# PEER experts of a hybrid decoder step: five places for gathered rows, one raw buffer for U, the row of sums in the memory of the h row, splits of U at other places

## The reference

```python
e = i1 * N_KEYS + i2                      # expert of the token, head and place, of 128 * 128
g = jax.nn.softmax(cv, axis=-1)
a = jax.nn.gelu(jnp.einsum('td,thkd->thk', tb, u_tab[e]).astype(jnp.float32), approximate=False)
return jnp.einsum('thk,thkd->td', (g * a).astype(tb.dtype), v_tab[e])
```

## Time and profile before

| | |
|---|---|
| median of 3 runs | 3907.29 us (3895.41 to 3909.98) |
| the profiled execution's own time | 3909.41 us |
| its span, first to last instruction | 3907.8 us |
| TensorE busy | 3267.4 us (84%) |
| VectorE busy | 2644.8 us (68%) |
| GpSimd busy | 1591.6 us (41%) |
| ScalarE busy | 1348.8 us (35%) |
| mean granted TensorE clock | 0.929 |

### The profile page before, as it was taken

How to read it: one execution, slowest core, us unless ns; L and a number is a source line. 1 busy time by engine, 2 the same in 40 slices (tenths; PEclk the granted TensorE clock), 3 DMA queues, 4 the chain that set the end, 5 groups by cost and what they waited for, 6 DMA issues and landing times. The chain is left out here.

```text
span 3907.8 us, 58722 instructions
## 1 busy us (share of the span) xinstructions
PE 3267.4 (84%) x20561; PEld 2846.2 (73%) x20561; DVE 2644.8 (68%) x5883; ACT 1348.8 (35%) x3194; POOL 1591.6 (41%) x1343
## 2 busy tenths in 40 slices
PE   6999788566687975656699999999999999999994
PEld 3676455211277964555599999999999999999993
DVE  4224776110234799989688888888888888888885
ACT  3010566000221113879433323333323333333331
POOL 0010000000212444999645545545546455455450
PEclk8999899777788987888899999999999999999997
DMA  6632873999412122665688888888888888888883
GB/s 226 239 131 73 236 215 114 367 414 410 165 65 89 60 76 71 251 245 204 273 311 332 314 311 340 321 320 339 306 327 322 317 335 316 315 336 312 320 293 136
DMA packets 280369, 991.41 MB, mean 254 GB/s; under 512 B 21925, under 2 KB 139536, under 8 KB 215865
## 3 DMA queue, kind: packets, MB, share of 16 engines
q1 hardware_dynamic: 214648, 480.71, 34.0%
q0 software_dynamic: 62784, 469.88, 31.8%
q10 hardware_dynamic: 2752, 38.75, 2.6%
HBM read 909.52 MB, written 146.80 MB: 270 GB/s over the span
## 5 line engine op out<-in xcount | busy, mean ns | idle before, releaser
L2210 PE MATMUL e_pa<-k_hi_d,e_uh 128*128 128x320 f32 x2048 | 616.0, 314 | 77.7 <-DVE e_act L2371 62.1
L2211 PE MATMUL e_pa<-k_lo_d,e_uh 128*128 128x320 f32 x2048 | 605.5, 309 | 0.0
L2410 POOL DMA_INDIRECT e_uv<-peer_uv,k_g_idx x416 | 400.6, 963 | 498.2 <-DVE e_pY L2351 442.5
L2339 DVE CUSTOM_DVE_ANT_0 e_uv<-e_uv,e_h 128x1024 f32<-128x1024 f32 x416 | 504.2, 1212 | 61.3 <-DMA e_uv<-peer_uv,k_g_idx 60.6
L2351 DVE SCALAR_TENSOR_TENSOR e_pY<-e_uv,e_wts,e_pY 128x1024 f32<-128x1024 f32 x412 | 527.3, 1280 | 0.0
L2210 PEld LDWEIGHTS e_pa<-k_hi_d,e_uh 128*128 128x128 f32 x2048 | 385.5, 188 | 103.6 <-DVE e_act L2371 87.7
L2405 POOL TENSOR_TENSOR e_vl<-e_v,e_vh 128x1024 fp32r<-128x1024 f32 x128 | 308.9, 2413 | 294.5 <-ACT e_vh L2262 294.0
L2289 ACT ACTIVATE e_gel<-e_dots 128x1 f32<-128x1 f32 x416 | 83.4, 200 | 956.2 <-DVE e_dots L2339 953.4
L2232 PE MATMUL e_po<-e_ph,e_vh 128*128 128x320 f32 x2048 | 387.4, 311 | 16.8 <-DVE k_OT L2385 12.3
L2211 PEld LDWEIGHTS e_pa<-k_lo_d,e_uh 128*128 128x128 f32 x2048 | 385.7, 188 | 0.0
L2241 PE MATMUL e_po<-e_pl,e_vh 128*128 128x320 f32 x2048 | 384.0, 309 | 0.4
(11 more groups left out here) (332 smaller groups left out, 5868.9 us busy)
## 6 DMA issues: line engine op xcount, KB each, us to landing
k_kv<-kv_pages SPq DMA_DIRECT2D x128, 512.0 KB, 6.7
s_kv<-kv_state SPq DMA_DIRECT2D x32, 2048.0 KB, 17.3
e_v<-peer_uv SPq DMA_DIRECT2D x128, 512.0 KB
e_u<-peer_ut SPq DMA_DIRECT2D x126, 512.0 KB
s_g<-r_G SPq DMA_DIRECT2D x10, 4096.0 KB
k_OT<-s_g SPq DMA_DIRECT2D x64, 640.0 KB
v_win_sample<-state_v_win POOLq DMA_DIRECT2D x28, 1168.0 KB
k_win_sample<-state_k_win ACTq DMA_DIRECT2D x28, 1168.0 KB
```

What stands on the lines that cost most here:

```text
L2210: nc.tensor.matmul(pa[:, m % 2, 0:WD], uh[:, c % 2, k], keep.hi_d[:, k, cols], start=(k == 0), stop=False)
L2211: nc.tensor.matmul(pa[:, m % 2, 0:WD], uh[:, c % 2, k], keep.lo_d[:, k, cols], start=False, stop=False)
L2339: nc.vector.tensor_tensor_reduce(uv[:, r, 0:D], uv[:, r, 0:D], h[:], 1.0, 0.0, ALU.mult, ALU.add, dots[:, r:r + 1]).then_inc(row_dotted, 1)
L2410: nc.gpsimd.indirect_dma_start(uv[:, s % RING], None, io["peer_uv"], bass.IndirectOffsetOnAxis(ap=keep.g_idx[:, s:s + 1], axis=0),).then_i ...
```

## The change

It touches the expert stage alone.

- `RING` is 5: five places for gathered rows, and the gather of step s + 5 waits for the sum of step s. There is one more gather at the start.
- The raw U has one buffer. A load of U waits until `low_u` of the chunk just before is done. At the start ACT loads chunk 0 alone; SP loads chunks 1 and 2, each when the `low_u` before it is done, and only then waits for and loads G. The order of SP's loop is written anew.
- `grow` is `hrow`: the copy of the sums goes into the memory of the h row. The row of the tile after next is loaded only eight steps into a tile, when the store of the sums has landed.
- The splits of U (ACT) and their low parts (POOL) stand at m = 1 and 4 and at n = 0 and 6.

```diff
--- before.py
+++ after.py
@@ -2067,7 +2067,7 @@
 NQ = NK // CQ
 DOTS = CQ * NBD
 OUTS = NBD * KC
-RING = 4
+RING = 5
 SUMS = 2
 
 
@@ -2078,7 +2078,7 @@
         def sb(name, shape, dt=F32):
             return ctx.enter_context(nc.sbuf_tensor(name, shape, dt))
 
-        uu = sb("e_u", [P, 2, KC, P])
+        uu = sb("e_u", [P, KC, P])
         vv = sb("e_v", [P, 2, D])
         uh = sb("e_uh", [P, 2, KC, P], F32R)
         ul = sb("e_ul", [P, 2, KC, P], F32R)
@@ -2095,7 +2095,7 @@
         G = keep.rest[:, 0:4 * DT].rearrange("p (u h n) -> p u h n", u=2, h=2 * ND)
         Gt = G.rearrange("p u h (c t) -> p u h c t", c=2)
         hrow = sb("e_hrow", [P, D])[:]
-        grow = sb("e_grow", [P, D])[:]
+        grow = hrow
         acc = keep.acc
         pa = ctx.enter_context(nc.psum_tensor("e_pa", [P, 2, 512], F32))
         po = ctx.enter_context(nc.psum_tensor("e_po", [P, SUMS, 512], F32))
@@ -2103,7 +2103,7 @@
 
         h = ctx.enter_context(nc.psum_tensor("e_h", [P, D], F32))
 
-        u_in = [nc.alloc_semaphore(f"e_u_in{u}") for u in range(2)]
+        u_in = nc.alloc_semaphore("e_u_in")
         v_in = [nc.alloc_semaphore(f"e_v_in{u}") for u in range(2)]
         g_in = [nc.alloc_semaphore(f"e_g_in{u}") for u in range(2)]
         uv_in = [nc.alloc_semaphore(f"e_uv_in{u}") for u in range(RING)]
@@ -2166,6 +2166,9 @@
             def _(sp):
                 for u in range(2):
                     sp.dma_start(vv[:, u], vview[u]).then_inc(v_in[u], 16)
+                for c in range(1, 3):
+                    sp.wait_ge(ul_done, c)
+                    sp.dma_start(uu[:], uview[c]).then_inc(u_in, 16)
                 for n in range(2):
                     sp.wait_ge(keep.g_stored[n], 16 * ND)
                 for u in range(2):
@@ -2173,8 +2176,8 @@
 
                 def load_u(i, c):
 
-                    sp.wait_ge(ul_done, CQ * i + c - 1)
-                    sp.dma_start(uu[:, c % 2], uview[ds(CQ * i + c, 1)].rearrange("a p k e -> (a p) k e")).then_inc(u_in[c % 2], 16)
+                    sp.wait_ge(ul_done, CQ * i + c)
+                    sp.dma_start(uu[:], uview[ds(CQ * i + c, 1)].rearrange("a p k e -> (a p) k e")).then_inc(u_in, 16)
 
                 def load_g(i, c):
 
@@ -2186,14 +2189,12 @@
                     sp.wait_ge(vl_done, CQ * i + c - 1)
                     sp.dma_start(vv[:, c % 2], row(vview, CQ * i + c)).then_inc(v_in[c % 2], 16)
 
-                for c in (2, 3):
-                    load_u(0, c)
                 with sp.Fori(0, NQ - 1) as i:
-                    for load, c in ((load_v, 2), (load_u, 4), (load_v, 3), (load_g, 4), (load_u, 5), (load_v, 4), (load_v, 5),
-                                    (load_g, 6), (load_u, 6), (load_u, 7)):
+                    for load, c in ((load_v, 2), (load_u, 3), (load_v, 3), (load_g, 4), (load_v, 4), (load_u, 4), (load_v, 5),
+                                    (load_g, 6), (load_u, 5), (load_u, 6)):
                         load(i, c)
-                for c in (2, 3):
-                    load_v(NQ - 1, c)
+                for load, c in ((load_v, 2), (load_u, 3), (load_v, 3)):
+                    load(NQ - 1, c)
 
             @block.tensor
             def _(pe):
@@ -2250,10 +2251,10 @@
             @block.scalar
             def _(act):
                 def split_u(c):
-                    act.wait_ge(u_in[c % 2], 16 * (c // 2) + 16)
+                    act.wait_ge(u_in, 16 * c + 16)
                     if c >= 2:
                         act.wait_ge(dotted, NBD * (c - 2) + NBD)
-                    nc.scalar.activation(uh[:, c % 2], uu[:, c % 2], ACT.Copy).then_inc(uh_done, 1)
+                    nc.scalar.activation(uh[:, c % 2], uu[:], ACT.Copy).then_inc(uh_done, 1)
 
                 def split_v(c):
                     act.wait_ge(v_in[c % 2], 16 * (c // 2) + 16)
@@ -2266,8 +2267,8 @@
                     c, b = m // NBD, m % NBD
                     act.wait_ge(dotted, n + 1)
                     nc.scalar.activation(pa[:, m % 2, 0:WD], pa[:, m % 2, 0:WD], ACT.Gelu).then_inc(gelu_done, 1)
-                    if b == 1 and c < 2:
-                        split_u(CQ * i + 2 + c)
+                    if m in (1, 4):
+                        split_u(CQ * i + 2 + m // 4)
                     act.wait_ge(p_done, n + 3)
                     if i:
                         act.wait_ge(summed, OUTS * i)
@@ -2279,9 +2280,9 @@
                 def h_copy(t):
                     act.wait_ge(h_in, 16 * t + 16)
                     nc.scalar.activation(h[:], hrow, ACT.Copy).then_inc(h_ready, 1)
-                    if t < GP:
-                        act.wait_ge(h_ready, t + 1)
-                        h_load(t + 1)
+                    if t == 0:
+                        act.wait_ge(h_ready, 1)
+                        h_load(1)
 
                 def weigh(s):
                     r = slice(s % RING, s % RING + 1)
@@ -2297,18 +2298,22 @@
                             weigh(s)
                             if last_of(s) and s < STEPS - 1:
                                 h_copy(tile_of(s) + 1)
+                            if s % P == 8 and 0 < tile_of(s) < GP:
+                                act.wait_ge(grow_out, 16 * tile_of(s))
+                                h_load(tile_of(s) + 1)
                         s = sums_of(NR * i + j)
                         if s is not None and last_of(s):
                             t = tile_of(s)
                             act.wait_ge(row_added, s + 1)
-                            if t:
+                            if t < GP:
+                                act.wait_ge(h_ready, t + 2)
+                            else:
                                 act.wait_ge(grow_out, 16 * t)
                             nc.scalar.activation(grow, pY[:], ACT.Copy).then_inc(grow_done, 1)
                             act.wait_ge(grow_done, t + 1)
                             act.dma_start(io["s_go"][t], grow).then_inc(grow_out, 16)
 
-                act.dma_start(uu[:, 0], uview[0]).then_inc(u_in[0], 16)
-                act.dma_start(uu[:, 1], uview[1]).then_inc(u_in[1], 16)
+                act.dma_start(uu[:], uview[0]).then_inc(u_in, 16)
                 split_u(0)
                 split_u(1)
                 for n in range(2):
@@ -2322,8 +2327,8 @@
                             split_v(CQ * i + V_AT.index(m))
                         gathers(i, m)
                     for n in range(OUTS):
-                        if n in (0, 2) and i + 1 < NQ:
-                            split_u(CQ * (i + 1) + n // 2)
+                        if n in (0, 6) and i + 1 < NQ:
+                            split_u(CQ * (i + 1) + n // 6)
                         gathers(i, DOTS + n)
                 act.wait_ge(grow_out, 16 * (GP + 1))
 
@@ -2398,7 +2403,7 @@
             def _(pool):
                 def low_u(c):
                     pool.wait_ge(uh_done, c + 1)
-                    nc.gpsimd.tensor_tensor(ul[:, c % 2], uu[:, c % 2], uh[:, c % 2], ALU.subtract).then_inc(ul_done, 1)
+                    nc.gpsimd.tensor_tensor(ul[:, c % 2], uu[:], uh[:, c % 2], ALU.subtract).then_inc(ul_done, 1)
 
                 def low_v(c):
                     pool.wait_ge(vh_done, c + 1)
@@ -2427,14 +2432,14 @@
                     gather(s)
                 for i in range(NQ):
                     for m in range(DOTS):
-                        if m % NBD == 1 and m // NBD < 2:
-                            low_u(CQ * i + 2 + m // NBD)
+                        if m in (1, 4):
+                            low_u(CQ * i + 2 + m // 4)
                         if m in V_AT:
                             low_v(CQ * i + V_AT.index(m))
                         gathers(i, m)
                     for n in range(OUTS):
-                        if n in (0, 2) and i + 1 < NQ:
-                            low_u(CQ * (i + 1) + n // 2)
+                        if n in (0, 6) and i + 1 < NQ:
+                            low_u(CQ * (i + 1) + n // 6)
                         gathers(i, DOTS + n)
```

## The result

The changed kernel takes 3970.65 us (median of 4 runs, 3967.46 to 3974.03), the kernel before 3907.01 us beside it. The ratio of the runs is 1.0169, 95% interval 1.0146 to 1.0191. The forecast was 3874 us. It is 64 us slower, not 33 us faster.

What follows compares the result with a forecast made beforehand. PE was taken to bound the expert stage, so only its waits count. Terms A, B and C, -15.7 - 25 + 5.5 = -35 us against 3909.4 us, gave 3874 us; the forecast's own range was 3866 to 3889, with rivals 3858 to 3903.

Steps and rivals of the forecast that it cites:

- What bounds the kernel: Expert stage: PE, busy 96%, is the bound; time changes only through the few places where PE stands still.
- Term A: Split moved from m = 3 to m = 4: PE's m = 6 no longer waits, 32 x 0.49 = -15.7 us.
- the replay: One turn replayed with the moved split: pl of m = 4 ends at 2771.0, leaving 0.5 us to spare at m = 7.
- rival 2: At m = 4 POOL's low_v goes before DVE's waiting pl; PE's m = 7 2.0 us late, 3938 us; chance 0.07.
- Term B: Gathers, mainly the product of n = 7: five places and moved low_u end late rows; 27 us at most, -25 taken.
- One U buffer at zero: Loads of U with one raw buffer land in 4.2 to 6.7 us; cost zero, with ACT's idle time as cover.
- Rival 3: Single U buffer makes ACT late: two loads a turn landing 3 us behind, 77 us, 3951 us; chance 0.10.
- The h and sums row: h and sums sharing one row, four times in the stage: cost zero, with the engine's own order as cover.
- Term C: Start: later chunk 1 of U moves first act and PE's m = 2 by 4.7 to 7.2 us; +5.5, bounds 3 to 8.
- The sum: Whole kernel: -15.7 - 25 + 5.5 = -35 us against 3909.4 us, so 3874 us; ends -39.7 and -20.

Runs made afterwards that it cites:

- added wait: The changed kernel with POOL's low_v at m = 4 first waiting until POOL's own low_u is done: 3897.0 us, ratio 0.9977.
- move alone: The kernel before with one edit, the split of U at m = 3 moved to m = 4 on ACT and POOL: 3969.19 us, ratio 1.0163.
- four-place run: The changed kernel with the wait between low_u and low_v, and RING 4 in place of 5: 3994.01 us, ratio 1.0219.

## Why the prediction was wrong, point by point

- **What bounds the kernel**: right. PE is busy in 97% of the stretch from 2000 to 3000 us at 1.00 once the faults are out, and each change of the time was a wait of PE or the clock behind it.
- **Term A, the failed step.** The 0.49 us of m = 6 came, and the replay's times hold up to `pl` (asked for 22.4 us into the turn, 22.5 in the replay). "It waits until 2770.6 and ends at 2771.0" is what failed: the replay let `pl` in between `low_u` and the `low_v` behind it. It waited for both, 4.50 us, and 0.5 us of spare became 1.84 us of waiting. That is rival 2, with its mechanism, its place and its price (2.0 us a turn forecast, 2.11 measured), held at 0.07. The row that spoke against it was read as a rule of the queue. Its second POOL instruction reads what the first writes, so it had to wait for the end and left 0.08 us in between. `low_v` reads nothing of `low_u`'s and overlaps it by 0.06 us. The added wait shows that this difference decides here. The Trainium skill ("SBUF — State Buffer", Who interferes with whom) has the first to issue hold the pair for the whole instruction. The 2.16 us of `pl` with the wait agree; issue order alone would also have let `pl` go before `low_v`, and the 4.50 us don't agree with that: the measurement decides.
- **The price of rival 2** was 32 us short, the clock. Its 3938 us and these 32 make 3970. Nothing in the rows of before showed the clock fall inside the stage, and no wait of PE there was longer than 1.7 us.
- **Term B**: right, and in full. The waits went from 58.3 to 2.1 us. But the five places are not needed for it: with four places and both U buffers, moving the split from n = 2 to n = 3 does it. What five places alone would give wasn't tried.
- **One U buffer at zero**: wrong once the turn is short. The bounds of 4.2 to 6.7 us to landing were medians of other stages, and the load on DMA is not what sets them apart. The 128 loads with 6.7 us run from 621 to 976 us in the kernel before, and DMA is as busy there (0.86) as in the expert stage. In the changed kernel the U loads take 5.0 us in the median. The first row is a stretch of the kernel before (columns as in the earlier trace rows), the second the U loads of the changed one:

```profile
620.00:975.00 355.00, 226.51 (x1634) 91.19 (x1634) 73.14 (x241) 63.97 (x144) 7.55 (x15) 0.81 0.86 351
...
e_u<-peer_ut SPq DMA_DIRECT2D x127, 512.0 KB, 5.0
```

But the one issued 27.3 us into the turn takes 9.1 us (median of the turns), and it is the one that counts. With the added wait it took 10.9 us from issue to use; SP had issued a G and a V load and POOL three gathers in the 8.3 us before it. With four places it cost 97 us. Rival 3 (late U) named the mechanism. The cover was called ACT's idle time; what counted was POOL behind ACT, and the gathers behind `low_u`. At the measured 61.4 us a turn it was indeed free.

- **The h and sums row**: zero, with nothing in the waits against it (3.9 us in all for the copy of the sums). It wasn't tried alone.
- **Term C**: +5.5 forecast, +5.8 measured in the first turn, but by another way, and the closeness is luck. Counted from PE's first matmul the first `act` comes 8.3 us later (19.8 us, 11.5 before), over the bounds of 4.7 to 7.2. It isn't the h row or the gelu that holds it but the G load, which SP issues only after both U loads. The prediction names it, but takes its number from the landing of U:

```profile
1919.11 0.49 DVE L2376 TENSOR_TENSOR e_act<-e_pa,k_OT 128x320 f32<-128x320 f32 x1 [40.85 <-DMA k_OT<-s_g]
```

- **The sum**: its ends, -39.7 and -20 us against 3909.4, make 3870 to 3889, not 3866 to 3889. It changes nothing here.

## What to carry to other kernels

When an instruction is moved so that another reader of the same port follows it at once, count the waiting engine as held until the last of the row, unless a wait stands between them; and replay a moved step with the queue behind it, not alone. A spare of 0.5 us is no cover when the wait it has to take is one whole instruction of another engine. Free a buffer only with the landing time of a load at that place of the turn, with the same transfers ahead of it. A median doesn't do: rows of another stage, with DMA just as busy, were 4 us and more short.

## What the runs showed of the hardware

- A VectorE instruction with two SBUF inputs that waits for GpSimd is not let in between two GpSimd instructions that overlap by 0.06 us (4.50 us, all 31 turns after the first; 4.51 with the move alone), and is let in when a wait puts 0.14 us between them (2.16). Whether the gap is the whole rule stays open. In the output projection of the kernel before, VectorE's product of 32 columns came through within 0.63 us, 0.04 us after the first of two such GpSimd instructions ended, although they overlap by 0.04 us:

```profile
1085.71 4.68 POOL L1358 TENSOR_TENSOR o_wlo<-o_raw,o_whi 128x1024 fp32r<-128x1024 f32 x2
...
1087.48 0.63 DVE L1444 TENSOR_TENSOR k_OT<-k_OT,o_late 128x32 f32<-128x32 f32 x1
```

- A stand of PE of 1.8 us is followed by 3.4 us at the lower clock in 21 turns of the changed kernel and by none in the 10 others, with the same work around it; with the move alone in 14 of 31. The length of the stand doesn't settle it: in the four-place run the clock falls 18 times, but behind this stand of 2.61 us it stays at 1.00. What picks the turn stays open; the price was 1.5 us each time in the changed kernel. Behind the two stands of 1.7 us in the stage of the kernel before it did not fall.

```profile
2848.00:2851.00 3.00, 0.41 (x3) 0.41 (x4) 2.10 (x4) 0.50 (x2) 2.84 (x2) 1.00 0.89 374
2851.00:2854.00 3.00, 3.00 (x23) 3.00 (x22) 3.00 (x6) 0.50 (x2) 0.94 (x1) 1.00 1.00 320
```

- A U load of 512 KB took 10.9 us from issue to use with a G and a V load and three gathers issued in the 8.3 us before it, and 9.2 us when it was issued 3 us earlier, ahead of the V load.
